# Decode logits of four sequences in four column groups, squares summed by GpSimd, and another order of ScalarE's casts in a decode-step kernel

## The reference, cut to what matters

```python
# decode, per sequence: 1024 cached keys and the new one, 8 heads on 2 kv heads
logits = jnp.einsum('btngd,btsnd->btngs', qg, kg) * HEAD_DIM ** -0.5
p = jax.nn.softmax(logits, axis=-1)            # over the kept keys
o = jnp.einsum('btngs,btsnd->btngd', p, vg)
# both mixers
mix = jnp.concatenate([rms_norm(out_a, lw['gn_lru_g']),
                       rms_norm(out_b, lw['gn_att_g'])], axis=-1) @ lw['w_out']
x = x + g1[:, None, :] * mix
```

## Time and profile before

| | us |
|---|---|
| median of three launches | 1306.44 |
| the profiled execution | 1305.35 |
| its span, first to last instruction | 1303.6 |
| PE busy in the span | 1263.4 (97%) |
| DVE, POOL, ACT busy | 857.0, 733.3, 670.5 |

### The profile page before, as it was taken

The page is one execution under the profiler, slowest core; times in us unless marked ns, Lnnn a source line. Parts: engine busy times, 40 slices in busy tenths (PEclk is TensorE's granted clock), DMA queues, the critical chain, the costliest instruction groups (busy, mean ns, idle before and its releaser), DMA issues.

```text
span 1303.6 us, 25268 instructions
## 1 busy us (share of the span) xinstructions
PE 1263.4 (97%) x9537; PEld 1159.3 (89%) x9537; DVE 857.0 (66%) x1586; ACT 670.5 (51%) x1151; POOL 733.3 (56%) x473
## 2 busy tenths in 40 slices
PE   6899999999899999999999999999999999999998
PEld 4677999877766766999999999999999999999998
DVE  5777889889678848677973454555545553644595
ACT  5557988967777776455342343433334336211115
POOL 0242457990152103456587787887878857765620
PEclk8899999999899999999999999999999999999999
DMA  9722106542101127655322243523534268999633
GB/s 347 281 70 74 50 6 213 173 143 82 46 21 30 46 74 228 191 158 146 106 98 66 99 167 133 186 101 130 185 134 170 78 248 311 328 334 347 242 129 131
DMA packets 127274, 198.86 MB, mean 153 GB/s; under 512 B 16839, under 2 KB 100111, under 8 KB 116656
## 3 DMA queue, kind: packets, MB, share of 16 engines
q1 hardware_dynamic: 127008, 193.01, 43.0%
q10 hardware_dynamic: 144, 4.23, 0.8%
HBM read 144.07 MB, written 53.18 MB: 151 GB/s over the span
## 4 chain that ended last, share of the span: by engine, by line
PE 70%; DVE 8%; ACT 5%; POOLq 5%; POOL 3%; DVEq 2%; issue 2%; SPq 2%; ACTq 1%; DMA 1%
PE ps L3508 30%; PE ps L3528 15%; PE ps L3192 2%; PE ps L3206 2%; PE ps L3372 2%; ACT junk L1354 2%; PE ps L3374 2%; PE ps L3373 2%; PE ps L3181 1%; POOLq L1076 1%; DMA ada_shift<-in_ada_w 1%; DVE junk L2073 1%; PE ps L3182 1%; DVEq L2623 1%; PE ps L3325 1%
## 5 line engine op out<-in xcount | busy, mean ns | idle before, releaser
L3528 PE MATMUL ps<-input,down_H 128*128 128x258 f32 x1120 | 180.7, 283 | 1.5 <-DVE acc L2771 1.5
L3528 PEld LDWEIGHTS ps<-input,down_H 128*128 128x128 f32 x1120 | 154.5, 190 | 2.1 <-issue 1.1
L3508 PE MATMUL ps<-comb,opH 128*128 128x258 f32 x960 | 154.4, 283 | 0.0
L1170 POOL TENSOR_TENSOR opL<-wsum,opH 128x512 fp32r<-128x512 f32 x80 | 123.7, 1556 | 36.1 <-ACT opH L1690 32.7
L1690 ACT CAST opH<-wsum 128x512 fp32r<-128x512 f32 x80 | 49.6, 621 | 168.0 <-PE ps L3508 109.6
L3508 PEld LDWEIGHTS ps<-comb,opH 128*128 128x128 f32 x960 | 132.7, 190 | 0.0
L3508 PE MATMUL ps<-h2H,opH 128*128 128x258 f32 x640 | 129.0, 283 | 0.3 <-DVE h2L L2628 0.3
L3508 PE MATMUL ps<-h2H,opL 128*128 128x258 f32 x640 | 129.0, 283 | 0.0
L3508 PE MATMUL ps<-h2L,opH 128*128 128x258 f32 x640 | 128.6, 282 | 0.0
L1013 POOL TENSOR_TENSOR wL<-wraw,wH 128x1024 fp32r<-128x1024 f32 x28 | 70.1, 2504 | 86.9 <-ACT wH L1347 86.7
L2771 DVE TENSOR_TENSOR acc<-ps,acc 128x516 f32<-128x516 f32 x112 | 76.6, 694 | 61.7 <-PE ps L3528 61.2
(11 more groups left out here) (528 smaller groups left out, 3532.1 us busy)
## 6 DMA issues: line engine op xcount, KB each, us to landing
down_inputs<-staged SPq DMA_DIRECT2D x35, 1032.0 KB, 4.9
input<-down_inputs SPq DMA_DIRECT2D x35, 1032.0 KB, 7.1
adb<-in_ada_w SPq DMA_DIRECT2D x8, 2048.0 KB, 8.5
wraw<-in_w_out SPq DMA_DIRECT2D x24, 512.0 KB, 4.5
raw<-in_w_gate SPq DMA_DIRECT2D x10, 1024.0 KB, 6.5
raw<-in_w_up SPq DMA_DIRECT2D x10, 1024.0 KB, 5.2
down_block<-in_w_down SPq DMA_DIRECT2D x5, 2048.0 KB, 11.0
x_feature_major<-x0T ACTq DMA_DIRECT2D x1, 4128.0 KB, 15.2
```

The costliest lines, as they stand in the source:

```text
L1170: pool.tensor_tensor(opL[g % OPS][:], operand(v, p), opH[g % OPS][:].bitcast(F32), ALU.subtract).then_inc(s_wL, 1)
L3508: ins = mm(ps[:, sum_bank(v, p) + h, 0:HC], weight[s][:, k, :], token[:, k, h * HC:(h + 1) * HC], start=begins, stop=ends, skip_group_chec ...
L3528: ins = mm(ps[:, 2 * m + h, 0:HC], weight[:, f, cc], tok[:, f, part, h * HC:(h + 1) * HC], start=(f == 0 and weight is hi and part == 0), ...
```

## The change

`decode_logits` takes four sequences at a time. Each has 32 output rows of its own (a column group of PE) in banks 0 to 2, which now fill 128 rows; sequence 4r+q puts its 8 heads into rows 32q+8r. The transposed keys of four sequences lie side by side in a new `kbT`, which takes the place of what `xT` tiles 1 to 4 need later; so the first reload of `xT` shrinks from three tiles to one, and the second grows from two to four. The pages are transposed in the order 2, 3, 0, 1, 4, 5, 6, 7 through banks 4 and 6. The transposes of the probabilities (64 of now 128 rows, picked by `decode_rows`) become true products.

Of the attention's squares, POOL adds the first seven token tiles (128x896, three additions), and DVE only the last tile. ACT's list of casts is reordered around the key copies, and `high(U_OUT + 3)` now stands ahead of the Exp. On DVE `group_diagonals(1)` moves ahead of three `mix_low`.

```diff
+DECODE_ORDER = (2, 3, 0, 1, 4, 5, 6, 7)
+DECODE_BANK = (4, 4, 6, 4, 6, 4, 4, 4)
+DECODE_AFTER = {1: 1, 3: 2, 4: 3, 5: 4, 6: 7, 7: 8}
...
-            sp.dma_start(xT[:, 0:3, :], spill[:, 0:3, :]).then_inc(s_spill, 16)
+            sp.dma_start(xT[:, 0:1, :], spill[:, 0:1, :]).then_inc(s_spill, 16)
...
-            sp.wait_ge(s_dlg, NB + 1)
+            sp.wait_ge(s_dlg, 3)
             sp.wait_ge(s_spill, 32)
-            sp.dma_start(xT[:, 3:5, :], spill[:, 3:5, :]).then_inc(s_spill, 16)
+            sp.dma_start(xT[:, 1:5, :], spill[:, 1:5, :]).then_inc(s_spill, 16)
...
+            pool.wait_ge(s_gsq, LT + 2)
+            pool.tensor_tensor(earlier[0], earlier[0], earlier[1], ALU.add)
+            pool.wait_ge(s_gsq, 2 * LT)
+            pool.tensor_tensor(earlier[2], earlier[2], earlier[3], ALU.add)
+            pool.drain()
+            pool.tensor_tensor(earlier[0], earlier[0], earlier[2], ALU.add).then_inc(s_gse, 1)
...
             page_keys_out(2)
+            page_keys_out(3)
+            new_keys_out(0)
+            group_root(1)
             for n in range(LT):
                 mix_high(0, n)
-            page_keys_out(3)
-            group_root(1)
             page_keys_out(4)
+            high(U_OUT)
+            page_keys_out(5)
             for n in range(LT):
                 mix_high(1, n)
-            high(U_OUT)
+            page_keys_out(6)
...
-            page_keys_out(5)
+            page_keys_out(7)
+            new_keys_out(1)
+            for n in range(LT, KD):
+                mix_high(0, n)
             high(U_OUT + 1)
...
             high(U_OUT + 2)
+            high(U_OUT + 3)
...
             A(dlg[:], dlg[:], ACT.Exp, bias=dsm[:, 1:2], scale=SCALE, accum_out=dsm[:, 2:3]).then_inc(s_dex, 1)
-            high(U_OUT + 3)
...
+            def last_squares_added():
+                sq = gsq[1][:, :, (NTT - 1) * P:T]
+                dve.wait_ge(s_gsq, 2 * LT + 1)
+                V.tensor_tensor(sq[:, 0:2], sq[:, 0:2], sq[:, 2:4], ALU.add)
+                dve.drain()
+                V.tensor_tensor(sq[:, 0], sq[:, 0], sq[:, 1], ALU.add)
+                dve.drain().then_inc(s_gsm, 1)
...
-                    ins = mm(ps[0:64, c, 0:n], qb[:].rearrange("p b k -> p (b k)")[:, 64 * b:64 * b + 64],
-                             kbT[b % 2][:, n0:n0 + n], start=False, stop=(b == NB - 1))
+                    for q in range(4):
+                        first = 72 * (4 * r + q) - 8 * r
+                        ins = mm(ps[32 * q:32 * q + 32, c, 0:n],
+                                 qb[:].rearrange("p b k -> p (b k)")[:, first:first + 32],
+                                 kbT[:, q, n0:n0 + n], start=False, stop=(r == 1), skip_group_check=True)
...
-                tr(ps[:, 3, g * 64:(g + 1) * 64], dlg[:, g * P:(g + 1) * P], ident[0:64, 0:64])
+                mm(ps[:, 3, g * 64:(g + 1) * 64], dlg[:, g * P:(g + 1) * P], decode_rows, start=True, stop=True)
```

More of the change, by code:

```diff
@@ L785, in _ @@
             sp.wait_ge(s_gx, 9)
-            pages(kpg, "cache_k", s_pg, 3)
-            for c, b in enumerate((1, 2, 0)):
+            pages(kpg, "cache_k", s_pg, 1)
+            for c, b in enumerate((3, 0, 2)):
                 sp.wait_ge(s_lh, c + 1)
@@ L1143, in _ @@
                     q_stacked(n // NKV + 2)
+            earlier = [gsq[1][:, n, 0:(NTT - 1) * P] for n in range(LT)]
+            pool.wait_ge(s_gsq, LT + 2)
[4 more added lines that the diff above has]
+            pool.tensor_tensor(earlier[0], earlier[0], earlier[2], ALU.add).then_inc(s_gse, 1)
             for u in range(NU_LRU, U_FFN):
@@ L1436, in _ @@
             root(1)
-            A(dsm[:, 7:8], consts[0:64, C_ONE:C_ONE + 1], ACT.Sigmoid)
+            A(dsm[:, 7:8], consts[:, C_ONE:C_ONE + 1], ACT.Sigmoid)
             gate_r(2)
@@ L1609, in _ @@
             act.drain().then_inc(s_gr, 1)
-            page_keys_out(5)
+            page_keys_out(7)
+            new_keys_out(1)
+            for n in range(LT, KD):
+                mix_high(0, n)
             high(U_OUT + 1)
[L1612 to L1617, removed]
             high(U_OUT + 2)
-            A(dsm[:, 7:8], consts[0:64, C_ONE:C_ONE + 1], ACT.Exp)
+            high(U_OUT + 3)
+            A(dsm[:, 7:8], consts[:, C_ONE:C_ONE + 1], ACT.Exp)
             act.wait_ge(s_dmx, 1)
             A(dlg[:], dlg[:], ACT.Exp, bias=dsm[:, 1:2], scale=SCALE, accum_out=dsm[:, 2:3]).then_inc(s_dex, 1)
-            high(U_OUT + 3)
             for n in range(LT, KD):
@@ L2500, in _ @@
             dve.drain().then_inc(s_gv, 1)
-            for n in range(LT):
+            mix_low(0, 0)
+            group_diagonals(1)
+            for n in range(1, LT):
                 mix_low(0, n)
-            group_diagonals(1)
             mix_half(1, 0)
@@ L3334, in _ @@
             group_roots(0)
-            for b in range(1, NB):
-                pe.wait_ge(s_dke, 2 * b)
-                turned_pages(b)
-                if b == 3:
-                    group_sums(1, 4, NTT)
-                decode_logits(b - 1)
-                if b == 1:
-                    pe.wait_ge(s_gr, 2)
-                    tr(ps[0:80, 3, 0:P], lasts[:], ident).then_inc(s_lt, 1)
-                if b == 2:
-                    group_sums(1, 0, 4)
-                if b == 4:
-                    group_roots(1)
-            decode_logits(NB - 1)
+            turned_pages(1)
+            pe.wait_ge(s_gr, 2)
+            tr(ps[0:80, 3, 0:P], lasts[:], ident).then_inc(s_lt, 1)
+            pe.wait_ge(s_hd, NG)
+            turned_pages(2)
+            turned_pages(3)
+            group_sums(1, 0, NTT)
+            turned_pages(4)
+            decode_logits(0)
+            turned_pages(5)
+            pe.wait_ge(s_dke, 6)
+            group_roots(1)
+            turned_pages(6)
+            turned_pages(7)
+            decode_logits(1)
             def out_group(g):
@@ L3608, in table @@
     c[0:8, C_E8:C_E8 + 64] = np.repeat(np.eye(8), 8, axis=1)
-    c[0:64, C_E8T:C_E8T + 8] = np.repeat(np.eye(8), 8, axis=0)
+    c[:, C_E8T:C_E8T + 8] = [[r % 32 < 16 and r // 32 + r % 32 // 8 * 4 == b for b in range(8)] for r in range(P)]
     freq = (np.float32(500000.0) ** (-np.arange(HALF, dtype=np.float32) / np.float32(HALF))).astype(np.float32)
```

88 lines of the change are left out of this document (51 added, 37 removed).

## The result

The changed kernel takes 1312.2 us (median of six, 1308.6 to 1314.5) against 1307.0 us (1304.9 to 1309.5) before on the same chip: a ratio of 1.004, with an interval of 1.0029 to 1.0051. That is 5.2 us slower where 2.3 were forecast, and above the range. The profiled execution is the fastest of the six, 1308.55 us with a span of 1306.6 us.

The account below looks back on a forecast made before the run. PE was taken to set the pace. Logits -11.2, ACT's waits +6.8 and +4.4, transposes +1.2 and -0.2, a swallowed wait -0.3 make +0.7; with the clock's +1.6, +2.3 us: 1308.7 us, range 1303.0 to 1311.0.

Parts of the forecast that it names:

- what bounds: From 482.4 us PE works nearly without a gap and sets the pace; DVE and ACT are nearly full.
- the rounds: Logits on PE: two rounds of four sequences at 2.1 us each instead of 15.4 us, so 11.2 us come off PE.
- rival of serial column groups: In the logits the column groups run one after the other, 7.7 us a round: 1311.5 us; chance 0.10, shared with other causes.
- the first hold: Before the output projection ACT waits 2.6 us for unit 0's load; PE idles 2.4, 1.9 and 1.3 us: +6.8 us.
- the second hold: ACT waits for unit 3's load ahead of the Exp; PE stands from 514.7 to about 519.0 us: +4.4 us.
- the transposes: PE's transposes of the probabilities grow from 0.7 to 1.9 us, +1.2 us, and start 0.2 us earlier.
- the gain stays: Rival: unit 3's load may not hold the Exp, PE is ahead by 3.2 us: 1303.2 us; chance 0.13.
- POOL's wait: PE's 0.43 us wait at 537.96 us for POOL's low part of unit 5 is swallowed in part: -0.3 us.
- the clock term: PE's clock falls to 0.50 behind its idle time before the transposes of the probabilities: +1.6 us, 0 as other bound.

Follow-up runs that it names:

- Two edits that take this hold away by different means: Changed kernel with unit 3's cast behind the Exp, 1305.46 us; changed kernel with unit 3's load ahead of the value pages of sequences 2 and 3, 1307.44 us.
- second profile: Profile of the changed kernel run again with no edit: 1313.3 us, ratio 1.0047 to the kernel before.
- the kernel before and its variant: The variant is the kernel before with the cast of unit 3 ahead of the Exp's table load: 1309.21 us, ratio 1.002.
- the second hold filled whole: Changed kernel with eight unread products of 384 columns between the second output group and PE's wait for the probabilities: 1311.08 us, ratio 1.0028.

## Why the prediction was wrong, by its steps

**Right: what bounds, and the rounds.** 1.97 us a round (forecast 2.1, 1.92). The rival of serial column groups, from 5.5 us a round, is refuted.

**Right: the first hold.** With the profile 0.8 us later at the group sums, the cast of unit 0 was due at 497.6 and began at 497.32. The idle times were 2.17, 1.47 and 1.20 us for 2.4, 1.9 and 1.3. DVE's scalings took 2.21 us (forecast 2.2), its diagonals 1.53 for 1.36 (a slip of 0.2 us for 0.3). The 2.2 us for one of POOL's additions do not follow from the row that is named (2.69 us for 1024 columns make 2.35 for 896); they took 2.07, 2.09 and 3.01 us, hidden. That the second hold hides this one is shown by moving the first cast alone (1.005 for 1.0047).

**Right: the second hold, and that it takes the gain.** The cast of unit 3 was due at 514.6 and began at 514.74; the transposes were due at 519.8 and began at 519.89. Two edits that take this hold away by different means gave 7.8 and 5 to 6 us, so "the gain stays" failed because the hold is there. A small error inside: the issue of unit 3 was to come 1.0 us earlier through the smaller reload of `xT`, and came 0.3 us earlier from the group sums on (30.4 for 30.8 us), none of it through the reload: from the issue of units 0 to 2 to that of units 3 to 5 there are 17.56 us for 17.59. Nor is SP without a pause there, as the prediction has it: behind the reload its rows show nothing for 2.8 us, in both kernels. The load landed quickly in the first profile (4.0 us) and 4.3, 4.4 and 4.9 us after its issue in the other three, where the transposes came 0.8 to 1.0 us later than in the first.

**Right: the transposes.** 2.00 us for 0.70, +1.3 for a forecast of +1.2. Seven profiles of variants have the new form and no fall behind it. From the transposes on five of them take 785.0 to 785.2 us, the others 785.8 and 786.2. That is 0.7 us and more above the 784.35 of the profile that the sum was made against, for a forecast of 1.2 less the 0.43 us of POOL's wait. The size is no closer than that: the three profiles of the kernel before differ by 1.2 us in this part.

**Wrong: the clock term, +1.6 us.** This is the step that failed. I took one price, from the one place in the trace with a longer idle time, and a bound of nothing below it, but no bound above. Against 785.1 us without a fall the four profiles of the changed kernel took 786.7, 788.8, 788.5 and 788.3 us: the fall costs 1.6, 3.7, 3.4 and 3.2 us, 3.0 on average, each uncertain by up to 1 us, the spread without a fall. The clock bears these sizes out: PE lost about half of the time for which it worked at half clock, which makes 1.7, 4.0 (the clock fell 2.3 us before the second profile's idle time was over), 3.4 and 3.4 us. The first profile is the forecast almost to the tenth (1308.55 us, 3.2 over its counterpart, of which 0.8 lie ahead of the stage), and three of four cost twice as much. With the transposes up to a microsecond late on top, the four lose 3.9 us on average from the group sums to the end (828.3 for 824.4 us), where 2.3 were forecast: 3.0 for the clock where 1.6 were given, 0.5 for transposes that were to come 0.2 us earlier, and 0.4 for the rest behind them where 0.9 were given. That no fall is likely behind a short idle time was also read from one execution: 2.10 us in another place did bring one, and the wait of the earlier trace rows itself did in 8 of 18 profiles.

**Open.** The ratios say 5 to 6 us, the profiles 3.9 for the stage and what follows. Another 0.8 us lie ahead of the stage on average, within the spread that both kernels have there; the rest of the difference is not placed. In the wait at 408.9 us, far ahead of the change, the clock fell in one of the four profiles of the changed kernel (for 3.4 us) and in 8 of 14 of it and its variants, but in none of the four of the kernel before and its variant. The instructions there are the same; the profiles are too few to tell whether it is chance.

## What to carry to other kernels

A wait on an in-order engine is priced by all that stands behind it: one cast, moved from behind the Exp to ahead of it, lost 8 of the 11 us that another engine had saved. When an engine is sped up, ask which load its partners will reach before it has landed, and move the loads or the waiting instruction first. Idle time on TensorE that puts nothing late in itself can still cost several microseconds through the clock; a price from one row of one execution wants a bound at twice or three times its size.

## What the runs showed of the hardware

- **The price of an idle time varies.** Of the same instructions behind the same wait, the clock was at half for 3.4, 10.2, 6.8 and 6.8 us in four executions; with 7.32 us of idle time for 13.7 us. It fell behind 2.87 us and in one place behind 2.10 us, and did not behind 1.03, 1.20, nor behind 2.09 us in ten of eighteen profiles. Idle time is not all: at the first round it fell in four profiles with no more than 0.65 us of it ahead, behind transposes and one-column products. The Trainium skill ("TensorE: Matmul & The Clock Gate", "Why this matters for your kernels") warns of gaps in PE's work; these runs agree, and the clock fell here behind shorter ones than it warns of. With product work in the gap the clock stayed at 1.00 (the second hold filled whole).
- **Column groups.** Sixteen passes of 512 float32 columns over four groups of 32, with eight passes of one column, took 1.97 us, as long as a quarter of that work took in one group of 64 rows.
- **DMA issue.** A reload of one `xT` tile took 1.62 us to issue behind three weight loads, three tiles 1.44 us; the same weight load alone behind idle time took 0.37 us. Here the size of the transfer did not set the time of its issue.
- **A fall ahead of a wait is free.** Where the clock fell at the second round, PE waited 2.5 us for the probabilities; where it fell only at the first, 6.0 us. The transposes began within a microsecond of each other, counted from the group sums.
